# Block inversion in a gated DeltaNet layer: one product W'W in place of two, written back by predicated copies

## The reference

```
k_beta = k * beta
a_low = jnp.where(strict, jnp.einsum("bhnid,bhnjd->bhnij", k_beta, k) * gamma, 0.0)
rhs = jnp.concatenate([v * beta, k_beta * jnp.exp(decay)[..., None]], axis=-1)
sol = lax.linalg.triangular_solve(a_low + jnp.eye(CHUNK, dtype=f32), rhs,
                                  left_side=True, lower=True, unit_diagonal=True)
```

## Time and profile before

| | |
|---|---|
| median of 3 runs | 1817.25 us (1816.94 to 1817.81) |
| the profiled execution | 1816.72 us |
| its span, first to last instruction | 1814.9 us |
| PE busy | 1799.1 us, 99% |
| VectorE busy | 1091.4 us, 60% |
| ScalarE busy | 859.9 us, 47% |
| mean granted clock of TensorE | 0.999 |

### The profile page before, as it was taken

The page is one execution under the profiler, slowest core; times in us unless marked ns, Lnnn a source line. Parts: engine busy times, 40 slices in busy tenths (PEclk is TensorE's granted clock), DMA queues, the critical chain, the costliest instruction groups (busy, mean ns, idle before and its releaser), DMA issues.

```text
span 1814.9 us, 28443 instructions
## 1 busy us (share of the span) xinstructions
PE 1799.1 (99%) x10790; PEld 1469.6 (81%) x10790; DVE 1091.4 (60%) x1523; ACT 859.9 (47%) x1369; POOL 100.2 (6%) x81
## 2 busy tenths in 40 slices
PE   8999999999999999999999999999999999999998
PEld 6888787787787888888888888888888888888886
DVE  5577686767876677775555555555444455555454
ACT  6454455554644545554444444444433344444443
POOL 0021030030210000000000000000000000000100
PEclk9999999999999999999999999999999999999999
DMA  7544443444434544445656665555555555555554
GB/s 270 172 160 132 140 151 118 162 131 139 138 130 140 190 156 166 155 155 185 205 197 202 198 209 186 187 186 185 188 196 190 193 189 186 186 186 192 190 192 139
DMA packets 88121, 316.42 MB, mean 174 GB/s; under 512 B 9728, under 2 KB 10496, under 8 KB 87888
## 3 DMA queue, kind: packets, MB, share of 16 engines
q1 hardware_dynamic: 86608, 311.20, 52.0%
q0 software_dynamic: 832, 3.02, 0.4%
q10 hardware_dynamic: 576, 0.71, 0.1%
HBM read 312.79 MB, written 2.10 MB: 173 GB/s over the span
## 4 chain that ended last, share of the span: by engine, by line
PE 96%; DVE 3%; issue 1%; ACT 0%; DMA 0%; POOLq 0%; POOL 0%; ACTq 0%; DVEq 0%
PE acc L327 29%; PE acc L328 28%; PE acc L329 28%; PE J L384 1%; PE J L423 1%; DVE w_lo L1194 1%; PE J L415 1%; DVE cT L1225 1%; PE J L522 1%; PE J L574 1%; PE J L427 1%; PE J L391 1%; PE J L372 1%; PE J L536 1%; PE J L451 0%
## 5 line engine op out<-in xcount | busy, mean ns | idle before, releaser
L1194 DVE TENSOR_TENSOR w_lo<-raw,w_hi 128x1024 fp32r<-128x1024 f32 x584 | 713.5, 1227 | 514.5 <-ACT w_hi L794 513.2
L794 ACT ACTIVATE w_hi<-raw 128x1024 fp32r<-128x1024 f32 x584 | 617.7, 1063 | 645.1 <-PE acc L329 637.7
L327 PE MATMUL acc<-w_hi,hT_hi 128*128 128x512 f32 x1440 | 577.7, 401 | 0.4 <-DVE hT_lo L1212 0.4
L328 PE MATMUL acc<-w_lo,hT_hi 128*128 128x512 f32 x1440 | 562.4, 391 | 0.0
L329 PE MATMUL acc<-w_hi,hT_lo 128*128 128x512 f32 x1440 | 561.6, 390 | 0.0
L327 PEld LDWEIGHTS acc<-w_hi,hT_hi 128*128 128x128 f32 x1440 | 270.6, 188 | 64.9 <-issue 7.0
L329 PEld LDWEIGHTS acc<-w_hi,hT_lo 128*128 128x128 f32 x1440 | 270.6, 188 | 57.9
L328 PEld LDWEIGHTS acc<-w_lo,hT_hi 128*128 128x128 f32 x1440 | 270.9, 188 | 52.4 <-issue 1.0
L327 PE MATMUL acc<-w_hi,act_hi 128*128 128x512 f32 x512 | 199.3, 389 | 0.0
L329 PE MATMUL acc<-w_hi,act_lo 128*128 128x512 f32 x512 | 199.2, 389 | 0.0
L328 PE MATMUL acc<-w_lo,act_hi 128*128 128x512 f32 x512 | 199.2, 389 | 0.0
(11 more groups left out here) (234 smaller groups left out, 1346.4 us busy)
## 6 DMA issues: line engine op xcount, KB each, us to landing
raw<-weights SPq DMA_DIRECT2D x584, 512.0 KB, 3.3
xres<-x POOLq DMA_DIRECT2D x4, 512.0 KB, 6.0
xres<-x SPq DMA_DIRECT2D x3, 512.0 KB, 9.2
y<-nat SPq DMA_DIRECT2D x6, 256.0 KB, 3.7
fgain_sb<-fgain SPq DMA_DIRECT2D x1, 1024.0 KB, 5.4
masks_sb<-masks POOLq DMA_DIRECT2D x1, 576.0 KB, 7.7
xres<-x SPq DMA_DIRECT2D x2, 256.0 KB, 5.5
y<-nat ACTq DMA_DIRECT2D x2, 256.0 KB, 3.1
```

The costliest lines, as they stand in the source:

```text
L327: mm(o, aT_hi[:, kt, tok], w_hi[:, c % RING, w], start=first, stop=False)
L328: mm(o, aT_hi[:, kt, tok], w_lo[:, c % RING, w], start=False, stop=False)
L794: A(w_hi[:, slot], raw[:, slot], ACT.Copy).then_inc(hi_ready, 1)
L1194: tt(w_lo[:, slot], raw[:, slot], w_hi[:, slot].bitcast(F32), ALU.subtract).then_inc(lo_ready, 1)
```

## The change

X has its non-zero part below the diagonal and U above it, and with W = U + V the product W'W holds the correction of U in the block above and that of X in the block below. So `both` becomes `square`, with 16 matmuls of W by itself, and what the two subtractions did is done by predicated copies from that product under masks that pick the level's blocks (the masks of the level for B now carry the sign). The copy of V by ScalarE becomes an addition V + U on VectorE. At the last level ScalarE first copies U into `solve`, and VectorE writes the correction over it.

```diff
-PE_INV_V = (46, 49, 54, 67, 72)
-PE_INV_U = (48, 51, 61, 69, 75)
+PE_INV_V = (46, 50, 55, 67, 72)
+PE_INV_U = (48, 52, 61, 69, 75)
...
-ACT_INV = (21, 21, 24, 33, 37)
+ACT_SOLVE = 33
...
-DVE_INV = (20, 21, 29, 31, 34)
+DVE_W = (18, 22, 26, 31, 34)
+DVE_INV = (20, 24, 29, 31, 34)
...
-        masks = sb("masks_sb", [P, 4 * P + 12 * C])
+        masks = sb("masks_sb", [P, 4 * P + 16 * C])
...
+        def by_parity(a):
+
+            return a.rearrange("p (a b) c -> p b a c", b=2)
+
+        level_out = J[:, 0:2, 0:U * C // 2].rearrange("p b (a c) -> p b a c", c=C)
...
-            def both(n, done):
...
+            def square(done):
+
                 for a in range(U // 2):
...
+                    for b in range(2):
+                        for ck in range(2):
+                            w = mats[rows(ck ^ b), M_V, 2 * a + b]
+                            ins = mm(J[rows(ck), b, a * C:(a + 1) * C], w, w, start=True, stop=True)
                 ins.then_inc(done, 1)
...
-                        pe.wait_ge(vcopy, LEVELS * g + (lv + 1))
-                        both(LEVELS * g + (lv + 1), zpass)
+                        pe.wait_ge(w_ready, LEVELS * g + (lv + 1))
+                        square(zpass)
...
-                for lv in range(LEVELS):
-                    if h == ACT_INV[lv]:
-                        act.wait_ge(vpass, LEVELS * g + (lv + 1))
-                        A(mat(M_V).rearrange("p (a b) c -> p b a c", b=2),
-                          J[:, 0:2, 0:U * C // 2].rearrange("p b (a c) -> p b a c", c=C), ACT.Copy).then_inc(vcopy, 1)
+                if h == ACT_SOLVE:
+
+                    act.wait_ge(inv_done, LEVELS * g + (LEVELS - 1))
+                    A(solve[:, 0::2, 0], uq[:, 0::2], ACT.Copy)
+                    for r, at in halves():
+                        ins = A(solve[r, 1::2, 0], uq[at, 1::2], ACT.Copy)
+                    ins.then_inc(solve_set, 1)
...
+                for lv in range(LEVELS):
+                    if h == DVE_W[lv]:
+
+                        dve.wait_ge(vpass, LEVELS * g + (lv + 1))
+                        tt(by_parity(mat(M_V)), by_parity(uq), level_out, ALU.add).then_inc(w_ready, 1)
+                    if h == DVE_INV[lv]:
+
+                        dve.wait_ge(zpass, LEVELS * g + (lv + 1))
+                        lower, upper = low_level[lv].bitcast(U32), up_level[lv].bitcast(U32)
+                        V.copy_predicated(by_parity(mat(M_X)), over(lower, U, 2), level_out)
+                        if lv < LEVELS - 1:
+                            V.copy_predicated(uq[:, 0::2], over(upper, U // 2), level_out[:, 0])
+                            for r, to in halves():
+                                ins = V.copy_predicated(uq[to, 1::2], over(upper[r], U // 2), level_out[r, 1])
+                        else:
+                            dve.wait_ge(solve_set, g + 1)
+                            ins = V.copy_predicated(by_parity(solve[:, :, 0]), over(upper, U, 2), level_out)
+                        ins.then_inc(inv_done, 1)
```

More of the change, by code:

```diff
@@ L24 @@
 F32R = mybir.dt.float32r
+U32 = mybir.dt.uint32
 AX_X = mybir.AxisListType.X
@@ L115, in hybrid_trunk @@
         part = sb("part", [P, NT, 4])
-        align = sb("align", [P, 336])
+        align = sb("align", [P, 80])
         raw = sb("raw", [P, RING, CK * NB])
@@ L170, in hybrid_trunk @@
         ident, tri, chunk_ones, ones = (masks[:, i * P:(i + 1) * P] for i in range(4))
-        (tri64, eye64, low, upi, up, nlow1, nup1, *up_level) = (
-            masks[:, 4 * P + i * C:4 * P + (i + 1) * C] for i in range(12))
+        (tri64, eye64, upi, up, nlow1, nup1, *levels) = (
+            masks[:, 4 * P + i * C:4 * P + (i + 1) * C] for i in range(16))
+        up_level, low_level = levels[:LEVELS], levels[LEVELS:]
         conv_w = colp[:, 0:192].rearrange("p (k n c) -> p k n c", k=3, c=4)
@@ L240, in spare, with over @@
             return J[:, 2 * t:2 * t + 2, 2 * P:4 * P]
-        def over(a, n):
+        def over(a, n, b=None):
+            if b:
+                return a.unsqueeze(1).unsqueeze(1).broadcast_to([a.shape[0], b, n // b, a.shape[1]])
             return a.unsqueeze(1).broadcast_to([a.shape[0], n, a.shape[1]])
@@ L265, in hybrid_trunk @@
             sem(n) for n in ("rows_rhs", "rows_done", "arg_done", "exp_done", "mask_done"))
-        kk_done, kqp_done, kqm_done, at_ready, x0_link, xu_link, u0_ready, bt_ready, vpass, vcopy, zpass, inv_done, x_odd = (
-            sem(n) for n in ("kk_done", "kqp_done", "kqm_done", "at_ready", "x0_link", "xu_link", "u0_ready", "bt_ready", "vpass", "vcopy", "zpass", "inv_done", "x_odd"))
+        kk_done, kqp_done, kqm_done, at_ready, x0_link, xu_link, u0_ready, bt_ready, vpass, w_ready, zpass, inv_done, solve_set = (
+            sem(n) for n in ("kk_done", "kqp_done", "kqm_done", "at_ready", "x0_link", "xu_link", "u0_ready", "bt_ready", "vpass", "w_ready", "zpass", "inv_done", "solve_set"))
         qt_done, qt_copied = sem("qt_done"), sem("qt_copied")
@@ L417, in spread @@
                 ins.then_inc(done, 1)
-            def both(n, done):
[L421 to L427, removed]
-                for a in range(U // 2):
[L429 to L441, removed]
+            def square(done):
+                for a in range(U // 2):
+                    for b in range(2):
+                        for ck in range(2):
+                            w = mats[rows(ck ^ b), M_V, 2 * a + b]
+                            ins = mm(J[rows(ck), b, a * C:(a + 1) * C], w, w, start=True, stop=True)
                 ins.then_inc(done, 1)
@@ L1326, in gdn_step @@
                     stt(out=zs2, in0=zs2, scalar=1.0, in1=z_raw, op0=ALU.add, op1=ALU.mult).then_inc(silu_done, 1)
[L1327 to L1338, removed]
                 for c in range(NCH):
@@ L1788, in mask_constants, with level @@
     r, j = (p % C)[:, None], np.arange(C)[None, :]
-    small = [r <= j, r == j, r > j, r <= j, r < j]
+    small = [r <= j, r == j, r <= j, r < j]
     nlow1 = -((r // 2 == j // 2) & (r > j)).astype(np.float32)
     nup1 = -((r // 2 == j // 2) & (r < j)).astype(np.float32)
-    levels = []
-    for lv in range(LEVELS):
+    def level(lv, odd, even):
         s = 2 << lv
-        levels.append((r // (2 * s) == j // (2 * s)) & ((j // s) % 2 == 1) & ((r // s) % 2 == 0))
+        return (r // (2 * s) == j // (2 * s)) & ((odd // s) % 2 == 1) & ((even // s) % 2 == 0)
+    levels = [np.where(level(lv, j, r), -1.0, 0.0) for lv in range(LEVELS)]
+    levels += [np.where(level(lv, r, j), 1.0, 0.0) for lv in range(LEVELS)]
     parts = [np.eye(P), tri, same, np.ones((P, P)), *small, nlow1, nup1, *levels]
```

## The result

| | before | after |
|---|---|---|
| median | 1817.11 us (6 runs, 1816.85 to 1817.95) | 1829.08 us (6 runs, 1828.11 to 1829.73) |
| the profiled execution | 1816.72 us | 1829.73 us |
| its span | 1814.9 us | 1827.0 us |
| mean granted clock | 0.999 | 0.992 |

What follows compares the result with a forecast made beforehand. TensorE (PE), busy 99% of the span, was taken to bound the kernel. 1816.72 + 0.0 (saving against stall) + 0.4 (margins) + 3.9 (clock) = 1821.0 us, 1821.5 against the median; range 1815.5 to 1831.

Steps and rivals of the forecast that it cites:

- rival 2: Clock behind the `square` 4 stalls: all four fall at the upper price, 1828 us; chance 0.47 together with the forecast.
- PE's share: Inversion, `both` to `square`: 0.52 us (upper bound 0.63) instead of 1.56, 1.04 us saved a level, 20.8 us in all.
- VectorE's share and the stall: VectorE's queue from the end of `square` 3 to level 4's addition: PE stalls 5.2 us at `square` 4.
- The sum of a group: Each group's inversion: the stall gives back all that five levels saved, 4 x 0.0 us.
- The margins of levels 0 to 2: Write-backs before PE's next `spread`: margins of 0.1 and 0.3 us, then several; 0.1 us lost a group, +0.4 us.
- The clock after a stall: Behind the `square` 4 stalls: three falls in four groups at 1.3 us each, 3.9 us; ends 0 and 10.4.
- Rival 1: Behind the stalls: the clock stays at 2.4 GHz, 1817.7 us, no change; chance 0.25.
- Rival 3: VectorE's write-backs: a predicated copy is slower, say two cycles an element, 14 us, 1832; chance 0.16 together with Rival 5.
- Rival 4: VectorE's chain between `square` 3 and level 4's addition is shorter: up to all 20.8 us come, 1796.4; chance 0.12.
- Rival 5: `square`, both operands one tile, runs at two tiles' pace, 1.04 us: 10 us, 1828; chance 0.16 together with Rival 3.

Runs made afterwards that it cites:

- half of `both`: Kernel before with only the first 16 of the 32 matmuls of `both`, subtractions taken as minima, so half of each correction is left out; 1798.65 us, ratio 0.9897.
- kernel without a stall: Changed kernel with two VectorE table entries moved: taps of V at steps 28, 28, 30 and level 4's addition at step 33; 1799.55 us, ratio 0.9901.
- one tap early: Changed kernel with taps of V at steps 28, 30, 31 in place of 30, 31, 31; 1822.37 us, ratio 1.0025.
- taps first: Changed kernel with the clauses for the addition and predicated copies put back behind those of the taps and silu, tables unchanged; 1828.45 us, ratio 1.0056.

## Why the prediction came out as it did

Direction, mechanism and range held: 1821.5 was forecast with 1815.5 to 1831, and 1829.08 came. It is 7.6 us above the forecast, in the upper part of the range, and nearer to the number of rival 2. In the forecast the stall only cancelled the saving (0.0 us); that the kernel would be slower at all hung on the clock, 3.9 of its 4.3 us. The direction held by that term, though its size was off by more than two.

**PE's share** was mis-sized: `square` at 0.52 us, read from the first part of `both`. It takes 0.62, the upper bound that I had named. Inside `both` the second part starts 0.06 us behind the last start of the first, in one row with it; in the half of `both` the last of the 16 starts near 148.35 and the next product only at 148.50. The 0.52 us was the first part without such an end, which `square` has. What the engine does in those 0.15 us no run shows. PE's saving alone is 19.0 us by the run with half of `both`, and what is left of it in the kernel without a stall is 18.3, not 20.8. For the changed kernel this counts fully, 0.1 us a level.

**VectorE's share and the stall** was right: the order of VectorE's instructions, with durations from the trace before, gave 5.2 us at `square` 4, and 5.17, 5.16, 5.16 and 5.17 came. The chain was 10.40 us against 10.36 worked out. The predicated copies took 2.0 us where I had 1.9, and the handovers a little less. Taking one or more pieces of the queue away gives stalls of 3.5, 2.7, 1.0 and 0 us, so that the order is the cause is shown and not only read.

**The sum of a group** without the clock was to be 0.0 and was 0.54 us: 2.2 us in all, from `square`. **The margins of levels 0 to 2**, for which I gave 0.4 us, cost nothing: PE has no wait there, and four levels gave 3.70 us, four times 0.925.

**The clock after a stall** was the term that failed most: 3.9 us for three falls of 1.3, where the trace has four falls that cost 8.4 (8.8 by medians), some 2.1 each. Both factors were low. I took the fall 4.1 us after the last matmul of the kernel as the time that a fall needs; in the four stalls the granted clock fell between 2.3 us (551.0, after a last matmul that ended near 548.7) and 5.2 us after it (305.2, after 300.1), and in other kernels it fell behind stalls of 3.5, 2.7 and 2.5 us, and of 2.5 and 1.9 in a row. One sample out of a scatter had served me as a rule. And I took the price from the start of the kernel, 2.6 us at the lower level. The stretches were 3.4 to 6.8 us long, part of it within the stall, where it costs nothing. The Trainium skill's rule that I weighed ("TensorE: Matmul & The Clock Gate", "What's actually happening": throttled by default, released by activity) has its four falls here, and the trace agrees with it; the prediction's sum by it was the better one. Taken as a rule for every stall it would have been wrong: behind the stalls of 1.0 us the clock fell never, and behind those of 2.7 us once in four.

**The start** was not in the prediction: 1.4 us of the 12.1 in the profiled pair. The same section of that page of the Trainium skill says that the throttled stretch at the start of one kernel varies between runs; the traces here, one of each of ten kernels, have the rise at 11.9 to 15.2 us, and no two of one kernel to show it. For the medians it may be smaller; the other runs have no trace, so how much of their 12.0 us it holds stays open.

**The terms together.** Against the forecast, `square` added 2.2 us and the clock 4.5, the margins took 0.4 away, and the start added 1.4: 7.7 us, where 7.6 were missed. All but the smallest went the same way, so the errors did not cancel. The band that I gave the forecast alone, 1818.5 to 1826, does not hold 1829.08; the range of 1815.5 to 1831 does, since it was widened for rivals 2 to 5.

**The rivals.** Rival 1 (the clock stays) fell with the windows. Rival 2 (four falls at the upper price, 1828) was right in the four falls and wrong in its price of 2.6 us; that its number came within 1.1 us is luck, since `square` and the start made up for the price. Rival 3 is out: the largest copy takes 0.74 us against 0.69, not twice as long. Rival 4, a shorter chain, didn't happen, but its number was near for a kernel that makes it so: it gave 1796.4 without any stall, and with `square` at 0.62 us that is 1798.4; the kernel with two edited table entries has 1799.55. It is 1% faster than the kernel before, and 1.6% faster than the change as made. Rival 5 is out by the rows of `square`, whose two operands are one tile: 0.62 us (148.74 to 149.36), not 1.04, and the same as the 16 matmuls of the half of `both`, whose operands are two tensors.

## What to carry to other kernels

When the helper of a product moves to another engine that works in order, list everything that stands ahead of it in that engine's queue from the moment at which its input is ready, and compare the sum with the work that the product's engine has meanwhile; and do it for the third engine too, whose own results may be queued behind a new wait. Putting the waiting instructions behind all the work that used to cover the wait is not enough: that made two stalls out of one, and 1828.45 us. What helped was to take that work out of the stretch that TensorE waits for, the taps to earlier steps and the silu and a split behind the addition. A stall of TensorE can cost more than its length. Here stalls of 1.0 us did not, and those of 2.5 us and more did in some groups or in all: take the granted clock around a stall into the sum, and the scatter of when it falls as a range, not one sample.

## What was not expected of the hardware

- In the profiled executions the granted clock fell to 0.50 behind stalls of PE of 3.5 us (one tap early) and 5.2 us (the changed kernel) in every group, behind a stall of 2.7 us in one group of four, and behind two stalls of 2.48 and 1.91 us with 5.9 us of work between them in every group, there after PE had been working again for 0.8 to 1.3 us. Behind a stall of 2.48 us alone it fell in two groups of four in the one kernel with taps first, and in none in the other; behind stalls of 1.0 us never. It stayed down 3.4 or 6.8 us each time, which cost 1.6 to 2.8 us a fall.
- 16 matmuls of 64x64 over four tiles take 0.62 us between two products, and 0.52 when other 64x64 matmuls follow.
- A predicated copy from PSUM takes 0.72 to 0.74 us for 128x512, 0.43 for 128x256 and 0.45 for 64x256; the subtractions of the same shapes took 0.69, 0.41 and 0.42. That is some 6% more.
